# Spacing of the gate pieces between the NSA attention steps: 17/12 of a step in place of 4/3

## What is computed

```python
for l in range(2):
    xn = rms_norm(x, attn_norm[l])
    (nsa_q, kv_c, kv_s, kv_w, nsa_g, cq, ckv, k_rope_raw,
     gate_a, gate_b) = split_cols(xn @ w_in[l])
    o_a = nsa_attention(...)        # 8 heads, compressed, selected and window branch
    o_b = mla_attention(...)        # 8 heads, low-rank keys and queries
    merged = sigmoid(gate_a) * (o_a @ nsa_w_o[l]) + sigmoid(gate_b) * (o_b @ mla_w_o[l])
    x = x + merged @ w_out[l]
    x = x + square(relu(rms_norm(x, mlp_norm[l]) @ w_up[l])) @ w_down[l]
return rms_norm(x, final_norm)
```

## Time and profile before

| | us |
|---|---|
| median of 3 runs | 1520.73 |
| the profiled execution, its time | 1520.22 |
| its span, first to last instruction | 1518.4 |
| TensorE matmuls busy in the span | 1496.2 (99%) |
| VectorE busy | 892.4 (59%) |
| ScalarE busy | 718.1 (47%) |
| GpSimd busy | 438.4 (29%) |

### The profile page before, as it was taken

One profiled execution on the slowest core, in us unless ns is written; L12 is line 12 of the kernel. 1 busy time (PEld: TensorE's weight loads), 2 busy tenths in 40 slices (PEclk: granted clock), 3 DMA queues, 4 the chain that ended last, 5 costly groups with the idle time before them and its releaser, 6 DMA issues.

```text
span 1518.4 us, 21125 instructions
## 1 busy us (share of the span) xinstructions
PE 1496.2 (99%) x7332; PEld 1252.0 (82%) x7332; DVE 892.4 (59%) x1539; ACT 718.1 (47%) x1308; POOL 438.4 (29%) x459
## 2 busy tenths in 40 slices
PE   8999999999999999999999999999999999999998
PEld 6888888887888888888888888888888888888887
DVE  6875766767553544535557776667575535354453
ACT  6864777873431222222366557877544222122222
POOL 1302667773020101101021046777711101010111
PEclk9999999999999999999999999999999999999999
DMA  5343222125232332333223421212432332333223
GB/s 211 100 151 135 71 80 64 56 99 173 91 98 97 97 97 97 97 97 97 97 84 125 173 84 65 76 63 63 132 118 91 98 97 97 97 97 97 97 97 111
DMA packets 43362, 154.29 MB, mean 102 GB/s; under 512 B 5440, under 2 KB 5440, under 8 KB 43280
## 3 DMA queue, kind: packets, MB, share of 16 engines
q1 hardware_dynamic: 37296, 133.77, 27.2%
q0 software_dynamic: 5696, 18.94, 3.4%
q10 hardware_dynamic: 288, 0.52, 0.1%
HBM read 142.73 MB, written 10.49 MB: 101 GB/s over the span
## 4 chain that ended last, share of the span: by engine, by line
PE 86%; DVE 4%; ACT 4%; issue 3%; DMA 1%; POOL 1%; POOLq 0%; DVEq 0%; SPq 0%; ACTq 0%
PE G L1481 14%; PE G L1482 13%; PE G L1483 13%; PE O L1482 9%; PE O L1481 9%; PE O L1483 9%; PE O L1769 3%; PE T L1745 3%; PE S L1720 2%; PE T L1481 2%; PE T L1483 2%; PE T L1482 2%; ACT F L668 1%; PE O L1556 1%; DVE F L1422 1%
## 5 line engine op out<-in xcount | busy, mean ns | idle before, releaser
L616 ACT ACTIVATE wsplit<-stage 128x1024 fp32r<-128x1024 f32 x227 | 240.2, 1058 | 598.8 <-PE G L1483 270.7
L977 DVE TENSOR_TENSOR wsplit<-stage,wsplit 128x1024 fp32r<-128x1024 f32 x180 | 262.4, 1458 | 72.9 <-ACT wsplit L616 72.6
L602 POOL TENSOR_TENSOR F<-Y 128x512 f32<-128x512 f32 x64 | 68.5, 1070 | 637.4 <-DVE Y L1439 637.4
L1481 PE MATMUL G<-xg,wsplit 128*128 128x512 f32 x560 | 223.5, 399 | 7.4 <-DVE wsplit L1003 7.0
L1482 PE MATMUL G<-xg,wsplit 128*128 128x512 f32 x560 | 219.1, 391 | 0.0
L1483 PE MATMUL G<-xg,wsplit 128*128 128x512 f32 x560 | 219.0, 391 | 0.0
L1214 DVE CUSTOM_DVE_ANT_0 F<-S,F 128x512 f32<-128x512 f32 x192 | 93.6, 487 | 99.2 <-PE S L1720 68.2
L500 POOL TENSOR_TENSOR wsplit<-stage,wsplit 128x1024 fp32r<-128x1024 f32 x46 | 111.3, 2420 | 126.4 <-ACT wsplit L616 126.3
L787 ACT ACTIVATE F<-F,nmx 128x512 f32<-128x512 f32 x192 | 107.7, 561 | 66.3 <-DVE nmx L1214 64.8
L1481 PEld LDWEIGHTS G<-xg,wsplit 128*128 128x128 f32 x560 | 105.6, 189 | 28.9 <-DVE wsplit L1003 7.0
L1481 PE MATMUL G<-area,wsplit 128*128 128x512 f32 x320 | 124.7, 390 | 0.3
(11 more groups left out here) (292 smaller groups left out, 3049.4 us busy)
## 6 DMA issues: line engine op xcount, KB each, us to landing
stage<-units SPq DMA_DIRECT2D x229, 512.0 KB, 3.5
stage_n<-units_n SPq DMA_DIRECT2D x20, 512.0 KB, 3.9
gates<-Y POOLq DMA_DIRECT2D x32, 256.0 KB, 3.0
E<-gates POOLq DMA_DIRECT2D x24, 256.0 KB, 3.5
F<-gates POOLq DMA_DIRECT2D x8, 256.0 KB, 3.7
x<-x_in SPq DMA_DIRECT2D x3, 512.0 KB, 6.4
rope<-tables POOLq DMA_DIRECT2D x1, 768.0 KB, 6.2
out<-F SPq DMA_DIRECT2D x3, 256.0 KB, 2.1
```

The source lines that it names most:

```text
L602: pool.tensor_tensor(F[:, m % 2, :], Y[:, m % 2, :], Y[:, m % 2, :], ALU.mult)\
L616: act.activation(wslot(u)[:, 0, :], staged(u), ACT.Copy).then_inc(s_whin if u in SN else s_whi, 1)
L977: dve.tensor_tensor(wslot(u)[:, 1, :], staged(u), wslot(u)[:, 0, :], ALU.subtract)\
L1481: pe.matmul(dst, a(0), b(0), start=first, stop=False)
```

## The change

One number in the placement of the 36 pieces: piece n goes to step 11 + (n - 12) * 17 // 12 in place of 11 + (n - 12) * 4 // 3.

```diff
 for n in range(len(DURING) * PIECES):
-    at = FIRST_STEPS[n] if n < 3 * PIECES else 11 + (n - 3 * PIECES) * 4 // 3
+    at = FIRST_STEPS[n] if n < 3 * PIECES else 11 + (n - 3 * PIECES) * 17 // 12
     FILL[at].append((DURING[n // PIECES], n % PIECES))
```

## The result

The changed kernel takes 1524.66 us (median of 10 runs, 1523.83 to 1527.35), the kernel before beside it 1520.55 us (10 runs, 1519.64 to 1522.36). The ratio is 1.0026, 95% interval 1.0018 to 1.0034. So it is slower by about 4 us, clear of no change at all.

The account below looks back on a forecast made before the run. TensorE bounds the kernel, matmuls busy 99% of the span. Per layer -0.1 + 1.25 + 0.25 = 1.4 us, 2.8 for two, on 1520.22 gives 1523.0, plus 0.5 to the median's scale: 1523.5 us; 8-in-10 range 1520.5 to 1525.6.

Parts of the forecast that it names:

- third rival: Steps 39 to 45: ScalarE late too, keys' copy holds gate 13 about 1 us; 1525.5 us, chance 0.13.
- Steps 39 to 48: Gate 13's later split starts GpSimd's queue late, so TensorE waits in steps 42 to 48: 1.25 us a layer lost.
- GpSimd is 1.7 us late: Step 48's transposes: released by job 44's scaling at 237.6, wanted by TensorE at 235.9.
- Steps 56 to 60: MLA 1's split moves from 53 to 56, putting GpSimd work before the scaling of jobs 56 and 57: 0.25 us a layer lost.
- TensorE wants it at 9.9, GpSimd has it at 10.1: Job 56's scaling, needed in step 60, in us from step 56's start; bounds 0 and 0.6 us a layer.
- The end of NSA: Steps 58 to 64: waits of 59 and 60 go, those of 63 and 64 come; gain 0.1 us a layer.
- Elsewhere: Other splits and evictions move by one step and meet no bare pair; cost nothing.
- Faster: Rival: spread removes waits of steps 58 to 63, 41 and 43, GpSimd's queue not binding; 1517.5 us, chance 0.05.
- No change: Rival: queue late but TensorE absorbs more, only jobs 38 and 40 late, 0.4 to 0.9 us a layer; 1520.9 us, chance 0.2.
- Slower by more: The third rival: backlog also reaches steps 50 to 60, one more microsecond a layer; 1525.5 us, chance 0.13.

Follow-up runs that it names:

- Gate 15 alone: Kernel before with only gate 15's four pieces moved to steps 56, 57, 59, 60, MLA 1's weight split moving with them from 53 to 56: 1522.07 us.
- MLA 1 earlier: Kernel before with MLA 1's pieces in steps 63, 64, 66, 70 in place of 65, 66, 67, 71: 1523.20 us.
- the last experiment: Kernel before with only the last three pieces of gate 15 moved, to steps 55, 58, 61: 1518.36 us, ratio 0.9978.

## Why the prediction was right, and where it was not

The forecast of 1523.5 us was 1.2 us short of the median, inside its range; the sign was right. It called the loss 0.18% with the bound at 0.2; it was 0.26%. By that bound the median fell in "slower", to which I had given 0.41 against 0.54 for "same", though the interval (0.18 to 0.34%) does not settle it. The median is also nearer to the third rival's 1525.5 than to the forecast.

*Steps 39 to 48, +1.25 forecast, +1.27 measured.* The queue ended within 0.01 us of where I had it, by luck: it began 0.13 late and took 0.14 less than the 14.4 of my sum (236.33 - 222.07 = 14.26; the largest error is in the two query rests, 2.53 in place of 2.76). The waits stand in steps 42, 44, 45 and 48 as listed, and the late split alone costs more than all of that in the old spacing. I had weighed starts (14.4 us) against reported lengths (13.9), and 14.26 is nearer to the starts. The rows with their neighbours show why: the store was reported as 0.59 and followed at 0.66, the output rest 1.27 and 1.51. The Trainium skill (Perfetto Trace Analysis, "GPSIMD Engine Instruction") says to time GpSimd's instructions by start-to-start spacing. With these numbers the trace agrees.

But the step "GpSimd is 1.7 us late" reads as if putting GpSimd right would bring it all back. It would bring 0.45: with the split at 38 the stretch still loses 0.83. So the size of this term was right and its cause only in part. The third rival's mechanism, the keys' copy behind ScalarE in step 45, was there too, hidden under the queue's waits in the sum and visible only when the queue was early. So was its second part, the scaling of job 44 behind the later second split (gate 14's, step 48). I had both limits and took them for alternatives; they are parallel, and the longer one sets the time while the other sets what can be regained. The rival's criterion (L1481 of step 45 waiting over 0.5 us) was not met in the changed kernel (0.30) and met at once when the queue was repaired (0.80).

*Steps 56 to 60, +0.25 forecast, about +0.65 measured (0.25 in step 58, 0.4 in step 60).* This is the term that was mis-sized. "TensorE wants it at 9.9, GpSimd has it at 10.1": it came 261.59 - 251.05 = 10.54 after step 56's start. L500 began after 4.68 (4.6 forecast), but from it to the scaling it is 5.05 us, not 4.6: between the output rest and the store there are 0.6 us idle, for which the trace names only the output rest itself, where a scaling follows it after 0.24. It is no accident of one place: in all seven kernels in which the store follows an output rest, 0.60 or 0.61 us lie between them, in both layers. The timeline of GpSimd:

```profile
255.73 2.39 POOL L500 TENSOR_TENSOR wsplit<-stage,wsplit 128x1024 fp32r<-128x1024 f32 x1 [1.20 <-ACT wsplit L616]
258.21 1.28 POOL L512 TENSOR_TENSOR on<-F 64x512 fp32r<-64x512 f32 x1
260.09 0.59 POOL L506 DMA_DIRECT2D gates<-Y  x1 [0.60 <-POOL on L512]
260.78 2.37 POOL L495 TENSOR_SCALAR F<-F,rsum,gt 128x512 f32<-128x512 f32 x4
```

The other part I left out: the split also stands before L782 on ScalarE, and holds the transposes of 58 by that way, without GpSimd. Moving the split took both away (0.65 us), so in this kernel it is the cause. Gate 15 alone shows that a split in step 56 does not cost this everywhere.

*The end of NSA, -0.1 forecast.* That the waits of 59 and 60 go and those of 63 and 64 come was right: two rows of 0.63 and 0.23, +0.46 and +0.24 by steps, against -0.34, -0.31 and -0.10 in 59, 60 and 62 where MLA 1's split is out of the way. The gain is as small as forecast: with that split out of the way steps 58 to 64 wait 0.13 less than before. That both wait for VectorE holds directly for step 63; step 64 waits for GpSimd, and GpSimd for VectorE.

*Elsewhere, 0 forecast.* Steps 11 to 38 have 0.06 us more, 50 to 57 0.02, 65 to 70 none.

The sum is then 1.84 a layer where I had 1.4, 3.7 in both. The last 0.4 us of the medians' distance of 4.1 is not in the waits of layer 0; the fastest runs are 4.2 apart as well, and where this rest lies stays open.

*The rivals.* "Faster" fell: it needed the queue to begin 1.7 us sooner, and even 3.1 sooner (split at 38) the kernel is slower than before. The gains it counts on at NSA's end exist, but they need the pieces of the last gate alone. "No change" fell with the waits over 1 us in sum. "Slower by more" had the right mechanism in part: its limits are there, but nothing of them reaches steps 50 to 57 (+0.02).

## What to carry to other kernels

When work is placed by rules from a table, follow each rule's other outputs before the table's own aim: here two weight splits that followed the spacing of TensorE's pieces, each behind a head's output and a tanh on an in-order engine, made 60% of the loss (1.1 us a layer), and the spacing with its other moves the rest (0.74). Write down not only when the late queue delivers but what waits right behind it, for that sets what a repair is worth. And where waits stand at the end of a table, move the last few entries alone: pairs of bare steps with one filled step between (55, 58, 61) took 1.0 us a layer out of steps 58 to 64, most of what the even stretching of the whole table was to take away there, and left steps 39 to 49 as they were.

## What the chip did that I had not expected

In the changed kernel's profile the granted TensorE clock is at its lower level, 1.2 GHz, from 1030.2 to 1037.0, and nowhere else between the first 13 us and the last 4. The stretches around it, layer 1 (length, busy by engine, clock):

```profile
1023.60:1030.40 6.80, 5.26 (x36) 4.60 (x36) 5.36 (x17) 6.60 (x16) 5.74 (x8) 0.98 0.26 82
1030.40:1037.20 6.80, 6.80 (x26) 6.28 (x27) 3.54 (x10) 4.57 (x12) 4.06 (x7) 0.52 0.00 0
1037.20:1044.00 6.80, 6.80 (x39) 5.81 (x38) 3.84 (x13) 5.00 (x13) 4.74 (x5) 1.00 0.24 70
```

In the slow stretch 26 matmuls go where 39 go in the next, at the full clock. From step 71 to step 95 layer 1 takes 57.50 us, layer 0 takes 54.54: 3.0 us lost. Ahead of it TensorE had waited once, in step 70, for 1.9 us:

```profile
1029.07 0.20 PEld L1745 LDWEIGHTS T<-constf,F 128*128 128x128 f32 x2 [1.93 <-issue]
```

The same wait, of the same length, stands in layer 0 of that execution (279.25) and in both layers of the kernel before (276.49 and 1024.57), and there the clock stayed at 2.4 GHz. The profiles of four other kernels (the split at 38, gate 15 alone, MLA 1 earlier, both splits) have a fall of 3.4 us in layer 1 as well, starting between 1026.9 and 1028.8, at a cost of 1.3 to 1.5 us each; four more with that wait (split at 39, gate 13 at 46, MLA 1's split at 58, gate 15 at 55, 57, 60) have none, and neither has MLA 1 earlier with gate 15's pieces later, whose longest wait there is 1.83. With the low part on VectorE, where step 42 waits two microseconds as well (a bracket of 1.99), it falls after step 42 and after step 70 in both layers, four times:

```profile
226.90:230.30 3.40, 3.40 (x16) 3.21 (x16) 2.31 (x4) 2.58 (x8) 3.09 (x3) 0.50 0.00 0
```

So a wait of this size is followed by a slow stretch in some executions, and in others a wait of the same length is not. That would spread the runs of one kernel by 1.4 to 3 us, as they are spread (1523.83 to 1527.35 for the change), and would make a short wait dearer than itself. The times do go with the granted clock of each run: in the kernel before beside the last experiment, the runs at 0.998 and above took 1519.70 to 1521.59 us, those at 0.997 and below 1521.61 to 1525.79. But not every slow stretch stands behind this wait. The profile of the kernel before has one from 1508.7 to 1512.1, in the final norm, and that of the split at 39 one from 1514.4; from step 95 of layer 1 to TensorE's last matmul these two take 433.9 us where the twelve others take 432.2 to 432.4. The version with 55, 58, 61, in which step 70 waits 1.3 us in place of 1.9, has no fall in its profile before the last microseconds, its twelve runs lie within 1.9 us, and none has a granted clock under 0.998, where 8 of the 17 of the kernel before have. That this is why its median gained more than its waits is likely and not shown: each kernel has one profile. For a comparison at this size, sum waits in a layer without a fall, and take times over ten runs or more.
